# Halving the columns of each matmul in a streaming-encoder block: two passes over half of the tokens or output columns per weight unit

## The chip, the cores and the metric

The kernel runs on one core of a Trainium2 chip. The metric is the device time in microseconds of one execution, as the median of several runs. The core has a matrix engine (TensorE, PE in the rows; its weight loads stand apart as PEld), VectorE (DVE), ScalarE (ACT), GpSimd (POOL) and an engine for synchronisation that also issues transfers (SyncE, SP).

## The reference

One residual block in float32 for 512 tokens of width 2048:

```python
def hybrid_mixer(h, w_in, ...):
    proj = h @ w_in                       # q, k, v, forget logits, x_rnn, gate_rnn
    ...
    y_attn = forgetting_attention(q, k, v, log_f).reshape(B, S, D_ATTN)   # 16 heads x 64
    x_rnn = causal_dwconv(x_rnn, conv_rnn_w, conv_rnn_b)
    y_rnn = rg_lru(x_rnn, ...) * jax.nn.gelu(g_rnn)
    y = jnp.concatenate([rmsnorm(y_attn, norm_attn_out), rmsnorm(y_rnn, norm_rnn_out)], axis=-1)
    return y @ w_out

def conv_gated_mlp(h, w_gate, w_up, conv_ffn_w, conv_ffn_b, w_down):
    g = causal_dwconv(h @ w_gate, conv_ffn_w, conv_ffn_b)
    return (jax.nn.gelu(g) * (h @ w_up)) @ w_down       # hidden width 6144

h = rmsnorm(x, norm_mix_pre);  x = x + rmsnorm(hybrid_mixer(h, ...), norm_mix_post)
h = rmsnorm(x, norm_ffn_pre);  x = x + rmsnorm(conv_gated_mlp(h, ...), norm_ffn_post)
```

## The kernel before

Every operand of a large product is split into two parts of reduced precision, hi and lo, and `product` (its three matmuls are lines 1723 to 1725) adds hi x hi, hi x lo and lo x hi into one accumulation bank. A bank holds 128 rows by 512 columns.

Weights arrive in *units* of 128 x 1024 numbers: eight tiles of 128 x 128 (`UK = 8`). For each unit SyncE issues a transfer into `raw`, ScalarE makes the hi part (lines 561, 924 and 567, by stage), VectorE the lo part (lines 1015, 1589 and 1025) and signals `split_done`; TensorE waits for that, uses the unit and signals `unit_used`, which frees the split's buffer. Two buffers (three in the fast products) take turns.

The stages in order, with what TensorE does in each:

- the opening: 4 units in another order (`opening_unit`) and four direct calls of `unit`, which stay as they are
- the projection: for each of 8 pairs of heads five *tiles* of the output (k, q, the recurrent input, its gate, v; the order is written out by hand in `pair`). A `tile` is two units, one for each half of the input channels. In a unit a weight tile of 128 x 128 is the stationary side and 512 tokens of one channel tile (`act_hi`, `act_lo`) are the moving side: 8 products, 24 matmuls. Between tiles, and in the middle of some units (`middle`), stand the attention's scores, transposes and value products and the gates of the recurrence. Pair 1 is written out; pairs 2 to 7 are a loop, `pe.Fori(2, NP)`, with `NP = 8`
- the output projection: `out_opening` and one unit written out (unchanged), then `out_half` 27 times, 24 of them in a loop of 3 turns
- the feed-forward part: `OPEN` units that start four tiles at once (unchanged), 8 tiles by `tile`, and then the *fast products* for the other 42 hidden tiles: seven products of half size in place of eight, in which each matmul moves 256 tokens (`HS = 256`). They are unchanged
- the down projection: `down_unit`, 4 groups of 24 units. Here the tokens are stationary: for each of 4 blocks of 128 tokens (a bank each) and each of 2 hidden tiles (`kt`) the hidden activation `h_tokens` is loaded, and 512 output columns of the weights move. Each group's units 2 to 21 are a loop of ten turns; the last unit of all is `last_unit`, which goes bank by bank
- the end: norm, transposes back, residual and stores

## Time and profile before

| what | value |
|---|---|
| median of 3 runs | 2210.19 us (2208.95 to 2212.57) |
| the profiled execution | 2208.31 us |
| its span, first to last instruction | 2206.6 us |
| TensorE busy | 2188.2 us (99%), 13418 matmuls |
| weight loads busy | 1936.6 us (88%), 13418 loads |
| VectorE busy | 1530.0 us (69%) |
| ScalarE busy | 1002.1 us (45%) |
| mean granted TensorE clock | 0.999 |

Matmuls overlap in the pipeline, so TensorE's busy share says only that it was never empty. What one matmul costs is the distance from its start to the next one's.

### The profile page before, as it was taken

To read this page: it belongs to the slowest core of one execution; us is meant where nothing else is said; L and a number is where in the kernel's file an instruction comes from. 1 tells how busy PE (TensorE), PEld (TensorE's weight loads), DVE (VectorE), ACT (ScalarE), POOL (GpSimd) and SP (SyncE) were. 2 spreads that over 40 slices of the span, in tenths; PEclk is the share of its full clock that TensorE was granted. 3 is DMA by queue.
4 is the path that set the end of the run, shared out by engine and by line. 5 is a ranking of instruction groups with operands and counts; after the bars stand their busy time and mean duration, and the time that the engine had idled before them with its cause. 6 is when DMAs were issued, how large, how long until landed. Compare 5 with 4: busy or idle time off the path is not lost.

```text
span 2206.6 us, 34616 instructions
## 1 busy us (share of the span) xinstructions
PE 2188.2 (99%) x13418; PEld 1936.6 (88%) x13418; DVE 1530.0 (69%) x2022; ACT 1002.1 (45%) x1275; POOL 140.2 (6%) x207
## 2 busy tenths in 40 slices
PE   9999999999999999999999999999999999999998
PEld 7778888888788888999999999999997888888886
DVE  7776777778755887888888888888884444444445
ACT  5555555447322554444444444444443343343433
POOL 0000000000100001111111111111112000000000
PEclk9999999999999999999999999999999999999999
DMA  5222222222432436777777777777767322222243
GB/s 173 88 90 95 82 97 96 89 95 83 140 120 95 153 115 195 211 209 202 205 208 207 208 207 207 214 213 204 203 180 284 124 96 95 97 98 94 97 171 117
DMA packets 100397, 328.67 MB, mean 149 GB/s; under 512 B 12976, under 2 KB 20784, under 8 KB 100160
## 3 DMA queue, kind: packets, MB, share of 16 engines
q1 hardware_dynamic: 75456, 240.06, 31.5%
q0 software_dynamic: 22240, 82.36, 17.0%
q10 hardware_dynamic: 2592, 4.72, 0.6%
q8 instruction: 77, 1.26, 0.2%
q14 instruction: 32, 0.26, 0.0%
HBM read 306.09 MB, written 21.00 MB: 148 GB/s over the span
## 4 chain that ended last, share of the span: by engine, by line
PE 93%; DVE 4%; issue 2%; ACT 1%; DMA 1%; POOL 0%; DVEq 0%; ACTq 0%; SPq 0%; POOLq 0%
PE bank L1723 30%; PE bank L1725 30%; PE bank L1724 30%; PE bank L1782 1%; PE bank L1795 1%; DVE w_all L1015 1%; ACT w_all L561 0%; DVE x_b L1714 0%; DMA raw<-weights 0%; PE bank L1807 0%; PE bank L1806 0%; PE bank L1867 0%; DVE act_lo L1030 0%; PE bank L1753 0%; DMA h_t<-h_spill 0%
## 5 line engine op out<-in xcount | busy, mean ns | idle before, releaser
L1723 PE MATMUL bank<-act_hi,w_all 128*128 128x512 f32 (+1 forms) x1760 | 617.2, 351 | 3.5 <-DVE w_all L1015 2.2
L1725 PE MATMUL bank<-act_hi,w_all 128*128 128x512 f32 (+1 forms) x1760 | 612.3, 348 | 0.0
L1724 PE MATMUL bank<-act_lo,w_all 128*128 128x512 f32 (+1 forms) x1760 | 609.6, 346 | 0.0
L1723 PEld LDWEIGHTS bank<-act_hi,w_all 128*128 128x128 f32 x1760 | 330.6, 188 | 48.7 <-issue 2.8
L1725 PEld LDWEIGHTS bank<-act_hi,w_all 128*128 128x128 f32 x1760 | 330.5, 188 | 46.1
L1724 PEld LDWEIGHTS bank<-act_lo,w_all 128*128 128x128 f32 x1760 | 330.6, 188 | 43.8 <-issue 0.2
L1025 DVE TENSOR_TENSOR w_all<-raw,w_all 128x1024 fp32r<-128x1024 f32 x96 | 117.6, 1225 | 287.7 <-ACT w_all L567 287.7
L1723 PE MATMUL bank<-w_all,act_hi 128*128 128x512 f32 x768 | 302.8, 394 | 2.2 <-DVE w_all L1025 1.4
L1725 PE MATMUL bank<-w_all,act_lo 128*128 128x512 f32 x768 | 301.1, 392 | 0.0
L1724 PE MATMUL bank<-w_all,act_hi 128*128 128x512 f32 x768 | 298.1, 388 | 0.0
L1015 DVE TENSOR_TENSOR w_all<-raw,w_all 128x1024 fp32r<-128x1024 f32 x135 | 165.3, 1224 | 143.6 <-ACT w_all L561 141.9
L1723 PE MATMUL bank<-tsum,w_all 128*128 128x256 f32 x896 | 247.3, 276 | 0.0
L1724 PE MATMUL bank<-tsum,w_all 128*128 128x256 f32 x896 | 247.3, 276 | 0.0
L1725 PE MATMUL bank<-tsum,w_all 128*128 128x256 f32 x896 | 247.3, 276 | 0.0
L567 ACT ACTIVATE w_all<-raw 128x1024 fp32r<-128x1024 f32 x96 | 101.8, 1060 | 297.1 <-PE bank L1725 283.7
L561 ACT ACTIVATE w_all<-raw 128x1024 fp32r<-128x1024 f32 x135 | 142.5, 1056 | 178.0 <-PE bank L1725 177.8
L924 ACT ACTIVATE w_all<-raw_s 128x1024 fp32r<-128x1024 f32 x112 | 119.1, 1063 | 154.1 <-PE bank L1725 151.2
L1725 PEld LDWEIGHTS bank<-w_all,act_lo 128*128 128x128 f32 x768 | 144.1, 188 | 33.7
L1724 PEld LDWEIGHTS bank<-w_all,act_hi 128*128 128x128 f32 x768 | 144.2, 188 | 32.2
L1723 PEld LDWEIGHTS bank<-w_all,act_hi 128*128 128x128 f32 x768 | 144.4, 188 | 31.8 <-DVE w_all L1025 1.6
L1589 DVE TENSOR_TENSOR w_all<-raw_s,w_all 128x1024 fp32r<-128x1024 f32 x112 | 137.3, 1226 | 46.6 <-ACT w_all L924 45.4
L1724 PEld LDWEIGHTS bank<-tsum,w_all 128*128 128x128 f32 x896 | 168.2, 188 | 0.0
(274 smaller groups left out, 3687.5 us busy)
## 6 DMA issues: line engine op xcount, KB each, us to landing
raw<-weights SPq DMA_DIRECT2D x310, 512.0 KB, 3.5
raw_s<-weights SPq DMA_DIRECT2D x84, 512.0 KB, 4.5
raw_s<-weights POOLq DMA_DIRECT2D x84, 512.0 KB, 6.1
raw_a<-weights SPq DMA_DIRECT2D x42, 512.0 KB, 5.2
h_spill<-h_out POOLq DMA_DIRECT2D x48, 256.0 KB, 3.6
h_t<-h_spill POOLq DMA_DIRECT2D x24, 512.0 KB, 7.6
x<-xT POOLq DMA_DIRECT2D x16, 256.0 KB, 3.1
out<-x ACTq DMA_DIRECT2D x16, 256.0 KB, 2.8
```

What stands on the lines that cost most here:

```text
L561: act.activation(w_hi[s], raw[:, s], ACT.Copy).then_inc(hi_done, 1)
L567: act.activation(wd_hi[s], raw[:, s], ACT.Copy).then_inc(hi_done, 1)
L924: act.activation(w_slot(q)[0], RAW_OF[n](i), ACT.Copy).then_inc(hi_done, 1)
L1015: dve.tensor_tensor(w_lo[s], raw[:, s], word(w_hi[s]), ALU.subtract).then_inc(split_done, 1)
L1025: dve.tensor_tensor(wd_lo[s], raw[:, s], word(wd_hi[s]), ALU.subtract).then_inc(split_done, 1)
L1589: dve.tensor_tensor(lo, RAW_OF[n](i), word(hi), ALU.subtract).then_inc(split_done, 1)
L1723: pe.matmul(dst, ah, bh, start=start, stop=False, skip_group_check=goes_on)
L1724: pe.matmul(dst, ah, bl, start=False, stop=False, skip_group_check=goes_on)
L1725: return pe.matmul(dst, al, bh, start=False, stop=stop, skip_group_check=goes_on)
L1782: last[e] = pe.matmul(dst, q, k, start=t == 0, stop=t == 2)
L1795: last = pe.transpose(dst, sm[:, c:c + P], ident[:])
```

## The change

`unit_by_tokens` is new. It takes the place of `unit` in `tile` and `out_half`: the unit's eight products are run over tokens 0 to 255 and then over tokens 256 to 511, each time with all eight weight tiles; what stood in the middle of the unit now stands between the two passes. `down_unit` and `last_unit` go bank by bank, and in each bank over output columns 0 to 255, then 256 to 511. The arithmetic is the same; each matmul of 512 columns becomes two of 256 into the two halves of the same bank, and its weight tile is loaded twice.

```diff
+            def unit_by_tokens(u, s, half, bank, start, stop, middle=None):
+                pe.wait_ge(split_done, u + 1)
+                for n in range(2):
+                    c = slice(HS * n, HS * n + HS)
+                    if middle and n:
+                        middle()
+                    for i in range(UK):
+                        k = half * UK + i
+                        last = product(bank[:, c], w_tile(s, i), (act_hi[:, k, c], act_lo[:, k, c]),
+                                       start and n == 0 and i == 0, stop and n == 1 and i == UK - 1, True)
+                last.then_inc(unit_used, 1)
+
             def tile(u, bank, between=None, middle=None, middle2=None):
 
-                unit(u, 0, 0, bank, True, False, middle=middle)
+                unit_by_tokens(u, 0, 0, bank, True, False, middle)
                 if between:
                     between()
-                unit(u + 1, 1, 1, bank, False, True, middle=middle2)
+                unit_by_tokens(u + 1, 1, 1, bank, False, True, middle2)
...
             def out_half(t, s, half, middle=None):
                 u = t * 2 + (N_OUT + half)
-                unit(u, half, half, OUT_BANKS[s][half], True, True, middle=middle)
+                unit_by_tokens(u, half, half, OUT_BANKS[s][half], True, True, middle)
...
             def down_unit(n, s, out_banks, start=False, stop=False):
                 pe.wait_ge(split_done, n + (N_HID + 1))
                 pe.wait_ge(h_split, n + 1)
-                for kt in range(2):
-                    w = slice(S * kt, S * kt + S)
-                    for i, bank in enumerate(out_banks):
-                        last = product(bank[:], (h_tokens(act_hi, s, kt, i), h_tokens(act_lo, s, kt, i)),
-                                       (wd_hi[s][:, w], wd_lo[s][:, w]), start and kt == 0, stop and kt == 1)
+                for i, bank in enumerate(out_banks):
+                    for c in range(0, S, HS):
+                        for kt in range(2):
+                            w = slice(S * kt + c, S * kt + c + HS)
+                            last = product(bank[:, c:c + HS], (h_tokens(act_hi, s, kt, i), h_tokens(act_lo, s, kt, i)),
+                                           (wd_hi[s][:, w], wd_lo[s][:, w]), start and c == 0 and kt == 0,
+                                           stop and c > 0 and kt == 1, True)
                 last.then_inc(unit_used, 1)
```

`last_unit` is changed in the same way as `down_unit`.

The first place is TensorE's program in the pair loop, around the gates in the middle of a unit of the third tile, `tile(u + 4, SB[1])` (bank3 is the tile's bank, bank5 and bank6 the gates'; a row is a matmul, and its weight load isn't shown). Before:

```order
L1723 MATMUL bank3<-act_hi,w_all 128x512
L1724 MATMUL bank3<-act_lo,w_all 128x512
L1725 MATMUL bank3<-act_hi,w_all 128x512
L1723 MATMUL bank5<-xc_hi,gw_hi 128x512 [waits xc_split,gw_split,pt_split]
L1724 MATMUL bank5<-xc_lo,gw_hi 128x512
L1725 MATMUL bank5<-xc_hi,gw_lo 128x512
L1723 MATMUL bank6<-xc_hi,gw_hi 128x512
L1724 MATMUL bank6<-xc_lo,gw_hi 128x512
L1725 MATMUL bank6<-xc_hi,gw_lo 128x512
L1723 MATMUL bank3<-act_hi,w_all 128x512
L1724 MATMUL bank3<-act_lo,w_all 128x512
```

And the same place with the change:

```order
L1723 MATMUL bank3<-act_hi,w_all 128x256
L1724 MATMUL bank3<-act_lo,w_all 128x256
L1725 MATMUL bank3<-act_hi,w_all 128x256
L1723 MATMUL bank5<-xc_hi,gw_hi 128x512 [waits xc_split,gw_split,pt_split]
L1724 MATMUL bank5<-xc_lo,gw_hi 128x512
L1725 MATMUL bank5<-xc_hi,gw_lo 128x512
L1723 MATMUL bank6<-xc_hi,gw_hi 128x512
L1724 MATMUL bank6<-xc_lo,gw_hi 128x512
L1725 MATMUL bank6<-xc_hi,gw_lo 128x512
L1723 MATMUL bank3<-act_hi,w_all 128x256
L1724 MATMUL bank3<-act_lo,w_all 128x256
```

The gates keep their shape and place. Ahead of them 12 matmuls of 512 columns have become 24 of 256, and as many stand behind them. In the pair loop's body, matmuls go from 310 to 550, and the other 24 instructions (registers, waits, the branch) stay.

The second place is TensorE's program in the down projection, across the wait between the first and the second unit of the first group. Before:

```order
L1723 MATMUL bank3<-w_all,act_hi 128x512
L1724 MATMUL bank3<-w_all,act_hi 128x512
L1725 MATMUL bank3<-w_all,act_lo 128x512
L1723 MATMUL bank0<-w_all,act_hi 128x512 [waits h_split,split_done]
L1724 MATMUL bank0<-w_all,act_hi 128x512
L1725 MATMUL bank0<-w_all,act_lo 128x512
L1723 MATMUL bank1<-w_all,act_hi 128x512
```

With the change:

```order
L1723 MATMUL bank3<-w_all,act_hi 128x256
L1724 MATMUL bank3<-w_all,act_hi 128x256
L1725 MATMUL bank3<-w_all,act_lo 128x256
L1723 MATMUL bank0<-w_all,act_hi 128x256 [waits h_split,split_done]
L1724 MATMUL bank0<-w_all,act_hi 128x256
L1725 MATMUL bank0<-w_all,act_lo 128x256
L1723 MATMUL bank0<-w_all,act_hi 128x256
```

The unit starts at the same bank behind the same wait, but stays on it for four products (12 matmuls) before it goes to the next one, where it went on after one product. The programs of the other engines are the same in both kernels.

## Rows read from the trace of the kernel before

**Rows 1.** The page: span, busy time by engine, TensorE's granted clock by slice

```profile
span 2206.6 us, 34616 instructions
...
PE 2188.2 (99%) x13418; PEld 1936.6 (88%) x13418; DVE 1530.0 (69%) x2022; ACT 1002.1 (45%) x1275; POOL 140.2 (6%) x207
...
PEclk9999999999999999999999999999999999999999
```

**Rows 2.** The page: the chain that ended last, by engine

```profile
PE 93%; DVE 4%; issue 2%; ACT 1%; DMA 1%; POOL 0%; DVEq 0%; ACTq 0%; SPq 0%; POOLq 0%
```

**Rows 3.** The waits (total us, times, longest): TensorE's two longest, ScalarE's on TensorE

```profile
PE bank L1867 <- POOL ones L472: 2.4, 1, 2.4
PE bank L1723 <- DVE w_all L1015: 2.2, 3, 1.1
...
ACT w_all L567 <- PE bank L1725: 283.7, 93, 4.5
```

**Rows 4.** Groups by line and shape on TensorE (busy us, mean ns | idle)

```profile
L1723 PE MATMUL bank<-act_hi,w_all 128*128 128x512 f32 x1088 | 431.7, 397 | 3.5 <-DVE w_all L1015 2.2 <-DVE act_lo L1364 0.7 <-DVE act_lo L1030 0.6
...
L1725 PE MATMUL bank<-w_all,act_lo 128*128 128x512 f32 x768 | 301.1, 392 | 0.0
...
L1723 PE MATMUL bank<-tsum,w_all 128*128 128x256 f32 x896 | 247.3, 276 | 0.0
...
L1723 PE MATMUL bank<-act_hi,w_all 128*128 128x256 f32 x672 | 185.5, 276 | 0.0
```

**Rows 5.** Busy time in stretches: PE, PEld, DVE, ACT, POOL, clock, DMA share, GB/s

```profile
900.00:1600.00 700.00, 700.00 (x6179) 700.00 (x6178) 576.08 (x699) 328.30 (x368) 86.40 (x111) 1.00 0.77 207
1700.00:2100.00 400.00, 400.00 (x1749) 328.23 (x1748) 179.40 (x158) 155.45 (x170) 3.39 (x5) 1.00 0.31 105
...
254.60:318.48 63.88, 63.88 (x312) 52.85 (x312) 46.19 (x80) 32.99 (x53) 1.07 (x2) 1.00 0.27 92
```

**Rows 6.** The timeline, TensorE: first and last of two runs of seven

```profile
1399.78 0.28 PE L1723 MATMUL bank<-tsum,w 128*128 128x256 f32 x1
...
1400.46 0.28 PE L1723 MATMUL bank<-tsum,w 128*128 128x256 f32 x1
...
1999.81 0.39 PE L1723 MATMUL bank<-w_all,act_hi 128*128 128x512 f32 x1
...
2001.18 0.39 PE L1723 MATMUL bank<-w_all,act_hi 128*128 128x512 f32 x1
```

**Rows 7.** The chain in order of time: start, us, what

```profile
80.00 1.05 ACT w_all L561
...
123.80 0.47 PE bank L1723
...
137.38 1.09 PE bank L1795 x10
...
538.81 1.06 ACT w_all L561
...
562.35 0.50 PE bank L1723
```

**Rows 8.** DMA: instruction queues of the whole; 210:540 us; 900:1600 us; issues

```profile
q8 instruction: 77, 1.26, 0.2%
...
q1 hardware_dynamic: 8544, 27.27, 24.5%
q0 software_dynamic: 912, 3.15, 3.1%
...
q8 instruction: 49, 0.80, 0.4%
...
par<-params SPq DMA_DIRECT2D x1, 168.5 KB, 3.5
...
negc<-tt POOLq DMA_DIRECT2D x1, 32.0 KB, 2.0
```

More of the change, by code:

```diff
@@ L2096, in last_unit @@
                 for i, bank in enumerate(out_banks):
-                    for kt in range(2):
-                        w = slice(S * kt, S * kt + S)
-                        last = product(bank[:], (h_tokens(act_hi, s, kt, i), h_tokens(act_lo, s, kt, i)),
-                                       (wd_hi[s][:, w], wd_lo[s][:, w]), False, kt == 1)
+                    for c in range(0, S, HS):
+                        for kt in range(2):
+                            w = slice(S * kt + c, S * kt + c + HS)
+                            last = product(bank[:, c:c + HS], (h_tokens(act_hi, s, kt, i), h_tokens(act_lo, s, kt, i)),
+                                           (wd_hi[s][:, w], wd_lo[s][:, w]), False, c > 0 and kt == 1, True)
                     last.then_inc(last_done, 1)
```

## The prediction

> **What bounds the kernel now.** I read the page's table of busy time first. TensorE is busy for 2188.2 of 2206.6 us, with 13418 matmuls, and its granted clock is in the top tenth in all forty slices [rows 1]; of the two levels, 1.2 and 2.4 GHz, that is the upper one. The share alone proves little, so the chain that ended last comes next: 93% of it is TensorE [rows 2]. The waits say the same from both sides. TensorE's own waits are few, the two longest 2.4 and 2.2 us in total, while ScalarE, which makes the first half of each weight split, waited 93 times for TensorE in the down projection, up to 4.5 us at a time, in a unit of 24 matmuls that lasts 24 x 0.229 = 5.5 us [rows 3]. The time is the number of matmuls times the distance from one start to the next, and the change touches just this product.
>
> **What a matmul costs.** The groups by line show two shapes: 3 x (1088 + 768) = 5568 matmuls of 512 columns, and 256-column ones in the fast products (quadrants of the activation and sums of quadrants) [rows 4]. The "mean ns of one" (392 and 276) isn't their price, since they overlap. The price is the spacing. In 900 to 1600 us TensorE never pauses and 6179 matmuls of 256 columns reach into the stretch; in 1700 to 2100 us it is 1749 of 512 columns [rows 5]. A matmul is counted when any part of it lies in the window, so the starts cover the window and one duration: 700.28 / 6179 = 113.33 ns, and 400.39 / 1749 = 228.93 ns. The timeline agrees as far as its digits go: six matmuls from 1399.78 to 1400.46 (113 ns each) and six from 1999.81 to 2001.18 (228 ns) [rows 6]. Two short ones cost 226.66 ns, one long one 228.93 ns: the long one is **2.27 ns dearer** than the pair that replaces it, though the pair needs a second weight load. That load shows no price of its own: in 900 to 1600 us loads are as many as matmuls, one each 113 ns, under busier DMA (0.77 against 0.31) and a busier VectorE (82% against 45%) [rows 5]. So contention doesn't explain why the long ones are dearer.
>
> The Trainium skill, in "TensorE: Matmul & The Clock Gate", section "Back-to-back issue gap", speaks against the change: it gives a spacing of N/2.4 + 2.5 ns, so each matmul has a fixed part and halving pays it twice. By that rule two of 256 would cost 2 x 109.2 against 215.8, 2.5 ns more, and the sum below would be +12.7 us, or 2223 us. The trace disagrees in both size and sign: 113.33 and 228.93.
>
> **The change part by part.**
>
> 1. *Which matmuls are split.* `tile` and `out_half` now call `unit_by_tokens`. Tiles: 10 units in each of the pairs 1 to 7 and 2 units of the first pair's last tile, 72 units, 1728 matmuls; the 8 tiles of the feed-forward part, 16 units, 384; `out_half` 27 times, 648. `down_unit` and `last_unit`: 96 units of 8 products of 3, 2304. Sum 5064 of the 5568; the other 504 (openings, direct calls of `unit`, `out_opening`) stay. TensorE should then show 13418 + 5064 = 18482 matmuls.
> 2. *Their price.* 5064 x 2.27 ns = 11.5 us less. Reading the row counts at the edge of the windows without that one duration gives 2.1 ns and 10.7 us; one more matmul or one less in 1749 moves it by 0.13 ns, 0.7 us. I keep 10.5 to 12.5 for the pure spacing.
> 3. *Where a faster TensorE brings nothing.* The chain leaves TensorE for a long stretch twice while split matmuls run: from 80.00 to 123.80 us (ScalarE and VectorE in the pair written out ahead of the loop) and from 538.81 to 562.35 us (the last head's work and the split of y) [rows 7]. There TensorE only arrives earlier at its wait. At most 67.3 / 0.229 = 294 split matmuls lie there: 0.7 us of the gain is given back as waits for VectorE. Nothing is queued behind those waits on TensorE but the matmuls of the same stage. Remaining: 10.8 us.
> 4. *The middle of a unit.* `middle` (gates, scores, transposes) ran after 12 matmuls of 512 and now runs after 24 of 256, which is 2.75 against 2.72 us into the unit. Cost nothing; the cover is that neither half has a wait of its own.
> 5. *Order in the down projection.* Before, four banks took turns and all ended in the unit's last quarter; now each bank gets its 12 matmuls in one piece. `unit_used` is signalled at the unit's end in both. `last_unit` already went bank by bank, so VectorE and ScalarE get the last four banks in the same rhythm. Cost nothing. The stationary side (tokens of h) is the same 128 columns, loaded once more.
> 6. *Other engines.* Their programs don't change. The tightest steady stage is the pair loop: VectorE has 46.19 us of work in 63.88 us [rows 5]. With 240 split matmuls a turn it becomes 63.3 us, and 17 us of slack are left on VectorE and 30 on ScalarE. In the down projection weights must come twice 5.5 us apart; transfers are asked for by the splits, which wait for TensorE, so everything moves up with it.
> 7. *Waits held in registers.* In the loops each unit is preceded by a register instruction and a wait (10 units in 6 turns, 8 in 3, 2 in 40: 164 of them). Before, the loop's stretch has the plain spacing, so they hide behind the 229 ns matmuls. They now have 113 ns cover from a single matmul. If all of this cover were needed they would cost up to 164 x 0.115 = 19 us; the nearest row is the fast stretch, where a wait stands before each 24 matmuls of 256 (written out, not looped) and costs nothing. I take nothing, being nearer to that, and keep the other end for the range.
>
> Sum: the profiled execution took 2208.31 us around its span of 2206.6. 2208.31 - 10.8 = 2197.5 (span 2195.8). The median of the runs is 2210.19, 1.9 us above that execution, so the forecast for a median is **2199.4 us**, 0.5% faster.
>
> **The rivals.**
>
> *Code loading (slower).* The pair loop's body grows from 310 matmuls with their loads and 24 other instructions, 644, to 1124. An instruction takes 0.80 MB / 12357 = 65 bytes, and the queue for instructions brings 1.26 MB / 77 = 16.4 KB a packet [rows 8], so the body grows from 2.5 to 4.4 packets' worth. Today it stays on the chip: from 210 to 540 us, five turns, no row for that queue appears [rows 8]. If 4.4 packets' worth no longer stays, each jump back (5 in the pair loop, 2 in the output loop, whose body becomes 3.1) waits for a transfer. Small transfers took 2.0 us and 3.5 us from issue to landing [rows 8]: 7 x 2.0 to 3.5 = 14 to 25 us, which makes 2213 to 2224 us. It decides from 1.6 us a jump. For it: nothing in the trace shows how much stays. Against it: what must stay only grows by two packets, and straight code never waits for it.
>
> The Trainium skill disagrees with itself here: "Advanced Engine Details and Errata", section "ISA Cache", gives TensorE 128 KB, in which 72 KB fit, and the same place and "Runtime: NRT & Kernel Launch", section "Instruction fetch mechanics", speak of two lines of 16 KB, outside which a taken branch stalls. The 2.5 packets that stay today are more than two lines, so the trace sides against the second.
>
> *A fixed cost per matmul in these stages (slower).* The 512-column spacing is 15.6 ns above 512 / 2.4; the 256-column one 6.7 above 256 / 2.4. If in these stages the 15.6 ns belonged to each matmul, through its place in the program and not its width, two would cost 244.5 ns and the time would be 2210.19 + 5064 x 15.6 ns = 2289 us. For it: ten transposes of only 128 columns take 1.09 us on the chain, 109 ns each, almost what 256 columns take [rows 7]. Against it: 672 x 3 matmuls of 256 columns read the very tensors act and w_all that the units read [rows 4], at the small spacing. From 1.1 ns per matmul on the gain is gone. The rule of the Trainium skill's TensorE page that is quoted above is a rival of this kind; its 2223 us is its time here.
>
> *The gain is eaten in part.* Points 3 and 7 larger than I took them: register waits at a third of their bound, or VectorE's stretches growing longer since the pair before ends sooner. 2203 to 2210, say 2206 us.
>
> *No effect.* That the change does nothing is excluded: the shapes change, and time can stay only if the costs cancel.
>
> **How the numbers follow.** Forecast 0.78, at 2199.4 with its own range of 2196 to 2202.5 (10.5 to 12.5 by spacing, and the runs' own scatter of about 2 us). Partly eaten 0.10. Code loading 0.07. Fixed cost 0.05. The range of 2195.5 to 2207.5 holds nearly all of the first and most of the second. A difference of under 0.2%, 4.4 us, can't be told from none: faster (under 2205.8) takes the first case and a third of the second, 0.81; same the rest of the second, 0.07; slower the last two, 0.12.
>
> **What would show it.** Right: in a stretch of the down projection 113.3 ns from start to start, some 3530 matmuls over 400 us where 1749 were; pair loop turns of 63.3 us in place of 63.88; granted clock unchanged; TensorE waits 0.7 us longer in all; some 90 instruction packets in place of 77. Wrong: instruction packets inside the pair loop and a pause of 2 us at its turns (code loading); a spacing above 114.5 ns in the units though the fast products stay at 113.3 (fixed cost); pauses at unit starts in loops only (register waits). If the long matmul's 228.93 ns came from the stage and not from its width, the spacing in the units would be half of it, 114.5 ns, and the time wouldn't move.

## The result: 1.2% slower, and the profile after

| what | value |
|---|---|
| median of 4 runs | 2236.26 us (2236.04 to 2237.01), before 2210.19 |
| ratio to before | 1.0116, 95% interval 1.0104 to 1.0128 |
| span of the profiled execution | 2234.4 us (27.8 longer) |
| mean granted TensorE clock | 0.999, as before |

The forecast was 2199.4 us. The page of the changed kernel answers to [rows 1, 2]:

```profile
span 2234.4 us, 44744 instructions
...
PE 2215.9 (99%) x18482; PEld 2176.5 (97%) x18482; DVE 1530.1 (68%) x2022; ACT 1002.7 (45%) x1275; POOL 140.5 (6%) x207
...
PEclk9999999999999999999999999999999999999999
...
q8 instruction: 91, 1.49, 0.3%
...
PE 92%; DVE 4%; issue 2%; ACT 1%; DMA 1%; SPq 0%; POOL 0%; DVEq 0%; ACTq 0%; POOLq 0%
```

The number of matmuls is the one forecast, VectorE and ScalarE do the work of before in the time of before, and the clock stayed at its upper level. The one large difference is in the weight loads: 88% before, 97% now. TensorE's waits are hardly longer than in [rows 3]:

```profile
PE bank L1723 <- DVE w_all L1025: 2.5, 1, 2.5
PE bank L1882 <- POOL ones L472: 2.4, 1, 2.4
PE bank L1723 <- DVE w_all L1015: 2.3, 3, 1.1
```

So the loss isn't in a wait, and must be in the spacing. The windows answer to [rows 5] (columns: stretch, its length, then busy time and count of PE, PEld, DVE, ACT and POOL, clock, DMA share, GB/s):

```profile
143.00:161.00 18.00, 18.00 (x161) 18.00 (x161) 10.61 (x22) 7.62 (x14) 0.54 (x1) 1.00 0.38 117
...
600.00:700.00 100.00, 100.00 (x852) 100.00 (x851) 53.67 (x69) 25.22 (x28) 3.23 (x6) 1.00 0.35 111
900.00:1600.00 700.00, 700.00 (x6179) 700.00 (x6178) 575.18 (x700) 328.78 (x367) 86.50 (x111) 1.00 0.79 208
1676.00:1685.00 9.00, 9.00 (x82) 9.00 (x81) 3.94 (x6) 2.09 (x3) 0.00 (x0) 1.00 1.03 393
1700.00:2100.00 400.00, 400.00 (x3398) 400.00 (x3398) 173.44 (x153) 149.36 (x164) 4.99 (x7) 1.00 0.32 103
256.83:321.51 64.68, 64.68 (x553) 63.84 (x552) 46.18 (x80) 33.11 (x53) 1.07 (x2) 1.00 0.30 91
```

With the counting of the prediction (a matmul lasts 0.28 us in these rows), the fast products still stand at 700.28 / 6179 = 113.33 ns. The down projection does not: 400.28 / 3398 = 117.80 ns, where 3530 matmuls were forecast. The output projection from 600 to 700 us has 100.28 / 852 = 117.70. Yet 143 to 161 us of the first pair, 18.28 / 161 = 113.5 (with the edges' roundness of one matmul, 0.7), and the first two units of the down projection, 9.28 / 82 = 113.2, have the shorter spacing in matmuls of the same lines and tiles. The pair loop's turn is 321.51 - 256.83 = 64.68 us instead of 63.88.

The timeline shows the two side by side, at the start of the third unit of the down projection (start, us):

```profile
1685.63 0.28 PE L1723 MATMUL bank<-w_all,act_hi 128*128 128x256 f32 x1
1685.74 0.28 PE L1724 MATMUL bank<-w_all,act_hi 128*128 128x256 f32 x1
1685.86 0.28 PE L1725 MATMUL bank<-w_all,act_lo 128*128 128x256 f32 x1
1686.42 0.38 PE L1723 MATMUL bank<-w_all,act_hi 128*128 128x256 f32 x1 [0.29 <-DVE act_lo L1019]
1686.64 0.28 PE L1724 MATMUL bank<-w_all,act_hi 128*128 128x256 f32 x1
1686.76 0.28 PE L1725 MATMUL bank<-w_all,act_lo 128*128 128x256 f32 x1
1686.88 0.28 PE L1723 MATMUL bank<-w_all,act_hi 128*128 128x256 f32 x1
...
1687.94 0.28 PE L1723 MATMUL bank<-w_all,act_hi 128*128 128x256 f32 x1
```

Ahead of the wait the starts lie 113 ns apart; behind it nine starts take 1687.94 - 1686.88 = 1.06 us, 118 ns each. Lines, tiles and shapes are the same on both sides, and the 118 ns go on to the end of the projection.

A matmul of 256 columns thus has **two spacings**, 113.3 and 117.8 ns. A pair at the shorter costs 226.7 ns, 2.27 less than one of 512 columns; a pair at the longer costs 235.6 ns, 6.7 *more*. Which of the two holds decides the sign. The time adds up with it: if all 5064 pairs had the longer spacing, the loss would be 5064 x 6.67 = 33.8 us. By the starts in the trace, each of the seven pairs of heads from the first on has one stretch at the shorter: six of 168 matmuls (84 pairs of matmuls each) and a last one of 72 (36), and in the down projection 96 have it (48). For 588 pairs x 8.94 ns that is 5.3 us less, so 28.5 us; the span grew by 27.8.

By stage, from starts in the two timelines: the fast products begin at 872.65 us instead of 860.19 (12.5 later), last from there to their last start 799.57 in both kernels (1672.22 - 872.65, 1659.76 - 860.19), and the down projection takes 2217.82 - 1674.98 = 542.8 us from its first start to its last instead of 2189.96 - 1661.45 = 528.5 (14.3 longer). Another 1.1 us is a longer wait ahead of it, for VectorE. The last starts, in the changed kernel and before:

```profile
2217.82 0.28 PE L1725 MATMUL bank<-w_all,act_lo 128*128 128x256 f32 x1
```

```profile
2189.96 0.40 PE L1725 MATMUL bank<-w_all,act_lo 128*128 128x512 f32 x1
```

### The profile page after: what moved, and what is told of

It is laid out like the page before. It is cut to its first block, busy times and chain, and to the rows that moved or that the text cites. A ratio compares the mean times of both kernels' runs of the same rounds, so it can differ in the third digit from the quotient of the medians.

```text
span 2234.4 us, 44744 instructions
## 1 busy us (share of the span) xinstructions
PE 2215.9 (99%) x18482; PEld 2176.5 (97%) x18482; DVE 1530.1 (68%) x2022; ACT 1002.7 (45%) x1275; POOL 140.5 (6%) x207
## 4 chain that ended last, share of the span: by engine, by line
PE 92%; DVE 4%; issue 2%; ACT 1%; DMA 1%; SPq 0%; POOL 0%; DVEq 0%; ACTq 0%; POOLq 0%
PE bank L1725 30%; PE bank L1723 30%; PE bank L1724 29%; DMA raw<-weights 1%; PE bank L1797 1%; DVE w_all L1015 1%; PE bank L1810 1%; ACT w_all L561 0%; DVE x_b L1714 0%; PE bank L1822 0%; DVE act_lo L1030 0%; PE bank L1821 0%; DMA h_t<-h_spill 0%; PE bank L1768 0%; DVE pt_lo L1109 0%
## 5 line engine op out<-in xcount | busy, mean ns | idle before, releaser
L1723 PE MATMUL bank<-act_hi,w_all 128*128 128x256 f32 (+1 forms) x2680 | 769.1, 287 | 3.6 <-DVE w_all L1015 2.3
L1725 PE MATMUL bank<-act_hi,w_all 128*128 128x256 f32 (+1 forms) x2680 | 764.0, 285 | 0.0
L1724 PE MATMUL bank<-act_lo,w_all 128*128 128x256 f32 (+1 forms) x2680 | 763.7, 285 | 0.0
L1723 PEld LDWEIGHTS bank<-act_hi,w_all 128*128 128x128 f32 x2680 | 502.9, 188 | 14.4 <-DVE w_all L1015 2.8
L1725 PEld LDWEIGHTS bank<-act_hi,w_all 128*128 128x128 f32 x2680 | 503.3, 188 | 6.9
L1724 PEld LDWEIGHTS bank<-act_lo,w_all 128*128 128x128 f32 x2680 | 502.8, 188 | 7.1 <-issue 0.2
L1723 PE MATMUL bank<-w_all,act_hi 128*128 128x256 f32 x1536 | 428.7, 279 | 2.8 <-DVE w_all L1025 2.5
L1725 PE MATMUL bank<-w_all,act_lo 128*128 128x256 f32 x1536 | 429.9, 280 | 0.0
L1724 PE MATMUL bank<-w_all,act_hi 128*128 128x256 f32 x1536 | 428.4, 279 | 0.0
L1025 DVE TENSOR_TENSOR w_all<-raw,w_all 128x1024 fp32r<-128x1024 f32 x96 | 117.7, 1226 | 301.6 <-ACT w_all L567 301.6
L1723 PEld LDWEIGHTS bank<-w_all,act_hi 128*128 128x128 f32 x1536 | 287.3, 187 | 3.2 <-DVE w_all L1025 2.7
L1724 PEld LDWEIGHTS bank<-w_all,act_hi 128*128 128x128 f32 x1536 | 288.8, 188 | 0.0
L1725 PEld LDWEIGHTS bank<-w_all,act_lo 128*128 128x128 f32 x1536 | 288.3, 188 | 0.0
```

Source lines behind the costliest of these rows:

```text
L1025: dve.tensor_tensor(wd_lo[s], raw[:, s], word(wd_hi[s]), ALU.subtract).then_inc(split_done, 1)
L1723: pe.matmul(dst, ah, bh, start=start, stop=False, skip_group_check=goes_on)
L1724: pe.matmul(dst, ah, bl, start=False, stop=False, skip_group_check=goes_on)
L1725: return pe.matmul(dst, al, bh, start=False, stop=stop, skip_group_check=goes_on)
```

## The experiments

The theories, in words: the matmul of 256 columns has two spacings and the units run at the longer one (the first theory of the expectations; with variants on what ahead of a stretch sets it); or the loss comes from a particular part of the change (passes, order in the down projection), from reading the same tensors that other engines write (contention), from the place in the program, or from semaphore waits. All kernels are made from the changed one; times of before are those of the same chip.

**One half of the change each.** `e1_tiles_only` keeps `down_unit` and `last_unit` of before; `e2_down_only` keeps `unit` in `tile` and `out_half`:

```diff
# e1
-                for i, bank in enumerate(out_banks):
-                    for c in range(0, S, HS):
...
+                for kt in range(2):
+                    w = slice(S * kt, S * kt + S)
# e2
-                unit_by_tokens(u, 0, 0, bank, True, False, middle)
+                unit(u, 0, 0, bank, True, False, middle=middle)
```

> Edit: the tiles and the output projection run by halves of the tokens as in the change; the down projection stays as before (512 columns). Theory 1 (two rhythms): a 256-column matmul runs either 113.3 or 117.8 ns from the next, and most of the changed units are in the slower one. 2760 long matmuls of 228.9 ns become 5520, of which 7 stretches of 168 ran at 113.3 in the changed kernel: 2760 x 6.7 ns less 1176 x 4.4 ns is 13 us, so about 2223 us. Theory 2 (the loss sits in the down projection alone, by its new bank order): 2210 us or less.

> Edit: the down projection as in the change; the tiles and the output projection as before. Theory 1: 2304 x 6.7 ns = 15 us more, less 0.4 us for the 96 matmuls at 113.3: about 2225 us, and the down projection at 117.8 ns a matmul but for its first two units. Theory 2 (losses add up only because both are changed, for instance by the code size): near 2210 us.

Measured: e1 2222.09 us, before 2209.11, ratio 1.0059 (1.0042 to 1.0075). e2 2223.39, ratio 1.0062 (1.0046 to 1.0079). Both halves lose, 13.0 and 14.3 us, 27.3 together, about the whole loss of 26 to 28 us: two losses of the same kind that add up, so no single place in the program is to blame. e2's windows hold a surprise:

```profile
1700.00:2100.00 400.00, 400.00 (x3399) 400.00 (x3398) 174.85 (x154) 151.42 (x166) 3.56 (x5) 1.00 0.32 100
2132.00:2200.00 68.00, 68.00 (x602) 68.00 (x602) 30.16 (x29) 25.70 (x27) 0.00 (x0) 1.00 0.27 85
```

From the eleventh unit of the last group on, behind a pause of 0.1 us at 2129.9 us, the spacing is 68.28 / 602 = 113.4 ns to the end (671 matmuls), while the changed kernel has the longer spacing in the same code (74 us from 2131 hold 631 matmuls, 117.7 ns).

**What a width costs.** `e3_forms` and `e8_widths` give feed-forward tiles 2 to 8 other cuts of their 512 columns (four tiles in e3, six in e8), each unit still once over all its weights per cut. The last of the seven keeps 256 and 256, and two tiles of e3 keep 256 columns in another order. Both kernels also take other orders in the groups of the down projection.

```diff
# e8
-            tile(N_FF + 12, PT[2])
+            tile_form(N_FF + 12, PT[2], ("cols", (0, 224, 512)))
-            tile(N_FF + 14, SB[2])
+            tile_form(N_FF + 14, SB[2], ("cols", (0, 248, 512)))
```

> Edit: the changed kernel with another form in each of the feed-forward tiles 2 to 8 (4 x 128 columns; 384 and 128; 448 and 64; 320 and 192; halves inside each product; halves inside each single matmul with the same weight tile twice in a row; 256 as in the change) and in each group of the down projection (512 as before; as in the change; both halves of a product one behind the other; all banks' first halves, then the second). Theory 1: every 256-column form shows 117.8 or 113.3 ns and nothing between, whatever its order, and which of the two changes at borders of units. Theory 2 (the order of banks and halves costs): the form whose order is that of before is at 113.3 or 114.5, the change's order alone at 117.8. The other widths show where the spacing stops following the columns: 128 columns near 109 to 113 ns if the weight load sets the floor, near 57 ns if the columns do.

> Edit: the changed kernel with other widths in the feed-forward tiles 2 to 8 (240 and 272; 224 and 288; 248 and 264; 208 and 304; 192, 192 and 128; 32 and 480; 256 and 256) and, by group of the down projection, both halves of a product one behind the other; all banks' first halves, then the second; as in the change; 512 columns. The run of other forms gave 108 to 112 ns up to 192 columns, and 15.5 ns above the column time (columns / 2.4) for 320 to 512. Theory 1: 256 columns lie where a floor of some 108 to 113 ns by the weight load meets the columns' line (106.7 + 15.6 = 122.3 ns), so widths up to 248 are at 108 to 113, and from 264 up (125.6, 129, 135.6, 142.3 ns) they follow the line. Theory 5 (15.6 ns is a cost of wide matmuls only): 264 to 304 columns at 6.7 ns above the column time (117 to 133 ns).

Measured once each: 2250.87 us (before 2209.11) and 2249.05 (2210.28). The whole times mix the forms; the spacings are what counts. In e8's timeline, the first start of each run of 24 matmuls of one width:

```profile
804.77 0.26 PE L1723 MATMUL bank<-act_hi,w_all 128*128 128x224 f32 x1
...
807.44 0.31 PE L1723 MATMUL bank<-act_hi,w_all 128*128 128x288 f32 x1
...
810.65 0.27 PE L1723 MATMUL bank<-act_hi,w_all 128*128 128x224 f32 x1
...
816.53 0.28 PE L1723 MATMUL bank<-act_hi,w_all 128*128 128x248 f32 x1
...
819.25 0.28 PE L1723 MATMUL bank<-act_hi,w_all 128*128 128x264 f32 x1
...
822.17 0.27 PE L1723 MATMUL bank<-act_hi,w_all 128*128 128x248 f32 x1
```

The difference of two starts divided by 24: 224 columns 111.3 ns, 248 113.3, 264 121.7, 288 133.8. The rest from the same two traces: 128 columns 111 to 112, 192 111, 208 110.8, 304 141.7, 384 175.4, and 512 stays at 228.9. So there are two regimes. Up to 248 columns the spacing is nearly a floor of 111 to 113 ns, whatever the width. Above 256 columns it is the columns at the upper clock level plus a fixed part: 264 / 2.4 + 11.7, 288 / 2.4 + 13.8, 384 / 2.4 + 15.4, 512 / 2.4 + 15.6. The width 256 stands at the corner, and its two spacings fit the two regimes: 113.3 is the floor as at 248, and 117.8 is 256 / 2.4 + 11.1, on the line to 264. The fixed part of the long matmul belongs to the matmul, and a pair pays it twice unless both run on the floor. That this is what the two spacings are is argued from the widths, not shown by itself.

e3 shows something else. Its last three tiles, with 256 columns in three orders, stand behind the tile of 320 and 192 columns, and all of them have the shorter spacing; its three groups of 256 columns in the down projection, in three orders too, have the longer one (PE, clock, DMA share, GB/s):

```profile
857.00:888.00 31.00, 31.00 (x276) 1.00 0.58 167
...
1840.00:2220.00 380.00, 379.26 (x3221) 1.00 0.32 103
```

31.28 / 276 = 113.3 ns, and 379.5 / 3221 = 117.8 (one pause taken off). The order sets neither.

The Trainium skill, "TensorE: Matmul & The Clock Gate", section "LDWEIGHTS (loading the stationary operand)", gives a load P / 1.2 ns, 106.7 for 128 columns, which is also 256 / 2.4. The floor measured here is 4 to 7 ns above that, and the loads' busy share of 97% in the changed kernel goes with it; that the loads set the floor is argued, no run takes them away. The rule that the prediction weighed, N / 2.4 + 2.5 in "Back-to-back issue gap" of the same page of the Trainium skill, is given there for an isolated matmul. It has the right sign; the constant is 11 to 16 ns in these traces.

**What moves a stretch from one spacing to the other.** `e4_nudge` puts small things ahead of units: one or two matmuls of ones, transposes, a first product cut in two (in the down projection at the heads of the second group, at 128 columns, and of the fourth, at 64).

```diff
+                            if cut and i == 0 and c == 0 and kt == 0:
+                                for c0, c1 in ((0, cut), (cut, HS)):
+                                    product(bank[:, c0:c1], (h_tokens(act_hi, s, kt, i), h_tokens(act_lo, s, kt, i)),
+                                            (wd_hi[s][:, c0:c1], wd_lo[s][:, c0:c1]), start and c0 == 0, False, True)
+                                continue
```

> Edit: the changed kernel with a small disturbance ahead of the feed-forward tiles 2 to 8 (one and two matmuls of ones, the first product cut at column 128 and at 64, one, four and ten transposes of 128 columns) and at the head of the down projection's groups 2 and 4 (first product cut at 128 and at 64). The order of the rest is the same. Theory 1 (two rhythms of the same stream, entered by the history of the pipeline): at least one disturbance moves the following matmuls from 117.8 to 113.3 ns, and they stay there until the next border. Theory 3 (the spacing is a property of the stage: its tensors, banks or what the other engines do there): every tile stays at 117.8.

Measured once: 2227.33 us, 9 less than the changed kernel, with more matmuls. In the feed-forward tiles no nudge changed anything. In the down projection (columns: PE, clock, DMA share, GB/s):

```profile
1700.00:1800.00 100.00, 100.00 (x851) 1.00 0.40 136
1820.00:2060.00 240.00, 240.00 (x2120) 1.00 0.30 96
2080.00:2130.00 50.00, 50.00 (x427) 1.00 0.48 175
```

Ahead of the first cut 100.28 / 851 = 117.8 ns, behind it 240.28 / 2120 = 113.3 through two whole groups, and behind the second cut 50.28 / 427 = 117.8 again. That lasts until a wait for VectorE at 2132 us, behind which the last 671 matmuls are at the shorter one, as in e2:

```profile
2134.00:2208.00 74.00, 74.00 (x656) 1.00 0.26 83
```

74.28 / 656 = 113.2 ns. A spacing is a **state that keeps itself up** through 2300 matmuls, waits in registers and banks changing, until something disturbs it.

`e5_lead_320` puts a product of 320 and 192 columns ahead in each unit, as what stood ahead of the three tiles of e3, in the expectation that it sets the shorter spacing.

```diff
+                for c in (slice(0, 320), slice(320, S)):
+                    product(bank[:, c], w_tile(s, 0), (act_hi[:, k, c], act_lo[:, k, c]), start and c.start == 0, False, True)
```

> Edit: the changed kernel, but each changed unit begins with its first product cut at column 320 (320 and 192 columns) and goes on by halves. In the run of other forms the stream was at 113.3 ns behind a tile of 320 and 192 columns. Theory 1a (the matmuls of 192 columns at the head bring the stream into the faster rhythm and it stays): most of the units at 113.3 ns, the time near 2200 us (2197 plus 211 heads that cost some 20 ns more each = 4 us). Theory 1b (the rhythm is drawn at each restart whatever stands ahead): a mix of both, 2205 to 2240 us. Theory 3 (a property of the stage): 117.8 throughout, 2240 us.

Measured: 2262.16 us, ratio 1.0234 (1.0217 to 1.0251). The matmuls of 256 columns in the units stayed at 117.8 ns, but for 21 in each of three turns of the pair loop, and there the next product of 320 columns ended the shorter spacing. That variant fell. The time lies above all the expectations, because the odd product costs more than the 20 ns put down for it. By the spacings of 320 columns (148.9 ns, the mean of e3's two runs of them) and 192 it is an estimated 3 x (148.9 + 111) - 6 x 117.8 = 73 ns, 15 us for 211 units; with the 5.3 us of the stretches at the shorter spacing that are gone, 5 of the 26 us stay unexplained.

**Contention, place, order, waits.** `e6_quiet_down` lets the splits of the down projection, from the third unit on, make one column instead of 1024: VectorE's and ScalarE's work there goes, and the output isn't the reference's.

```diff
-                act.activation(wd_hi[s], raw[:, s], ACT.Copy).then_inc(hi_done, 1)
+                c = slice(None) if isinstance(n, int) and n < 2 else slice(0, 1)
+                act.activation(wd_hi[s][:, c], raw[:, s, c], ACT.Copy).then_inc(hi_done, 1)
```

> Edit: the changed kernel; in the down projection the splits of all weights and hidden tiles but the first two units' make one column in place of all (so the output is not the reference's from there on); the transfers and signals stay. VectorE and ScalarE are nearly idle there, and the splits are ready early. Theory 3 (other engines' reads and writes stretch the 256-column matmuls to 117.8 ns): the down projection at 113.3 ns, 20 us less than the changed kernel, 2216 us. Theory 1: 117.8 or 113.3 as the entry falls, a group as a whole, and no spacing between the two; the 563 ns wait behind the second unit is gone, and if a wait is what moves the stream to the slower rhythm it stays at 113.3 until the next disturbance.

Measured once: 2235.51 us, and the longer spacing from the first unit of the down projection on. VectorE is busy for 29.27 us of 400 instead of 173.44, ScalarE 30.61 instead of 149.36, and TensorE has the same 3399 matmuls:

```profile
1700.00:2100.00 400.00, 400.00 (x3399) 400.00 (x3398) 29.27 (x154) 30.61 (x164) 4.26 (x6) 1.00 0.32 102
```

`e7_shift` runs 25 instead of 18 matmuls of ones at the very start; the program behind is the changed kernel's.

```diff
-            keep_busy(18, PT[2])
+            keep_busy(25, PT[2])
```

> Edit: the changed kernel with 25 in place of 18 matmuls of ones in the idle time ahead of the first product. Nothing else. Theory 1 (the rhythm falls with the timing of restarts): the stretches at 113.3 and at 117.8 ns may lie at other places than in the changed kernel, in steps of whole stretches; time within 2225 to 2240 us. Theory 4 (each place in the program has its own spacing, for instance by its address in the instruction stream): the same stretches as in the changed kernel, since the instructions behind move by 7 only; time 2236 us.

Measured once: 2239.23 us. The stretches that have the shorter spacing are others. The first feed-forward tile by `tile`, 783 to 797 us, in this kernel and then in the changed one:

```profile
783.00:797.00 14.00, 14.00 (x126) 1.00 0.25 78
```

```profile
783.00:797.00 14.00, 14.00 (x121) 1.00 0.35 105
```

14.28 / 126 = 113.3 ns against 14.28 / 121 = 118.0, in the same instructions. In turn the first two units of the down projection, and the first pair's stretch from 143 us, have the longer spacing in e7. So the place in the program alone doesn't choose. It isn't without effect, though: in the loop's six turns, in e7 and in each of the ten other profiled kernels whose pair loop runs its tiles in 256 columns alone, the shorter spacing begins behind the same four transposes and holds up to the next ones (168 matmuls, 72 in the last turn). Behind the same transposes in the first pair, ahead of the loop, it is there in eight of these kernels and missing in e4, e7 and e12. In e12, whose edit comes much later, TensorE's instructions up to there are those of the changed kernel, which has 161 matmuls in this window:

```profile
143.00:161.00 18.00, 18.00 (x155) 1.00 0.34 110
```

`e9_halves_inner` runs both halves of the columns in each product before the next weight tile; `e10_same_weights_twice` goes further, two halves behind each other on the same weights; `e11_wait_each_24` adds a semaphore wait in the middle of each unit, as the fast products have it at each 24 matmuls.

```diff
# e9
-                for n in range(2):
...
+                for i in range(UK):
...
+                    for n in range(2):
# e10
+                        for n in range(2):
+                            c = slice(HS * n, HS * n + HS)
+                            last = pe.matmul(bank[:, c], w, a[:, k, c], start=start and i == 0 and j == 0 and n == 0,
# e11
+                    if n:
+                        pe.wait_ge(split_done, u + 1)
```

> Edit: as the changed kernel, but the two halves of a product stand one behind the other (three matmuls of the first half, three of the second), in the tiles, the output and the down projection. The same number of 256-column matmuls. Theory 1 (two rhythms, fallen into at restarts, not by order): 113.3 and 117.8 ns again, in other stretches than in the changed kernel; anything from 2198 us (all fast) to 2239 us (all slow). Theory 6 (this order is what was fast in the run of other forms): 113.3 nearly throughout, 2198 to 2203 us.

> Edit: as before, but each weight tile's load is followed by its second use at once: hi x hi on both halves, then hi x lo on both, then lo x hi. Each matmul still loads its own. Theory 1: as for the run ahead, 2198 to 2239 us. Theory 7 (loading the tile that is already there costs less): below 113.3 ns a matmul, under 2195 us.

> Edit: the changed kernel with the unit's wait written a second time ahead of its second pass, so that a wait stands before each 24 matmuls, as in the fast products (which ran at 113.3 ns in every run so far). Theory 8 (that regular wait keeps the stream in the faster rhythm): the tiles and the output projection at 113.3 ns, the down projection as in the changed kernel; about 2219 us. Theory 1: no such effect, 2225 to 2240 us.

Measured: 2234.88 (ratio 1.0109, 1.0092 to 1.0126), 2236.60 (1.0119, 1.0102 to 1.0136), and once 2235.18 us. All three have 851 or 852 matmuls from 600 to 700 us and 3398 or 3399 from 1700 to 2100, as the changed kernel. Order, loading the same weights again, and waits that are met already don't matter; each trace is one execution, and e9's four runs, from 2231.97 to 2236.99 us, leave room for a stretch at the shorter spacing in some.

**Are the fast products immune?** `e12_disturb_fast` puts wide matmuls or transposes into the fast products of five of the 42 hidden tiles.

```diff
+                if n == 2 and i in (14, 32):
+                    for _ in range(2 if i == 14 else 8):
+                        pe.transpose(wide[:, 0:P], ident[:], ident[:])
+                if n == 2 and i == 26:
+                    for _ in range(3):
+                        product(wide[:, 0:320], (hi[:, 0:P], lo[:, 0:P]), (act_hi[:, 0, 0:320], act_lo[:, 0, 0:320]), True, True, True)
```

> Edit: the changed kernel with extra matmuls, whose results are overwritten, inside the fast products: one product of 512 columns ahead of the third product of tile 8, two transposes at 14, eight products of 512 at 20, three of 320 at 26, eight transposes at 32. Theory 1 (the fast products are at 113.3 ns because nothing disturbs them once they are there): behind one or more of these the stream is at 117.8 ns and stays there up to the next one, 504 matmuls x 4.4 ns = 2.2 us for each six tiles. Theory 9 (the fast products' own operands hold them at 113.3 ns): 113.3 within a few matmuls behind each disturbance; only the extra matmuls' own time, some 8 us, is added to the changed kernel's 2236 us.

Measured once: 2246.33 us. The products of 512 columns left the spacing as it was. Two transposes brought the next 46 matmuls to 117.8 ns, and with the first matmul on the third buffer (`w` in the names, where the others are `w_all`) it was 113.3 again:

```profile
1145.83 0.28 PE L1724 MATMUL bank<-tsum,w_all 128*128 128x256 f32 x1
...
1151.25 0.28 PE L1725 MATMUL bank<-tsum,w_all 128*128 128x256 f32 x1
1151.36 0.28 PE L1723 MATMUL bank<-act_hi,w 128*128 128x256 f32 x1
```

46 starts in 1151.25 - 1145.83 = 5.42 us, 117.8 ns each. Behind the 320-column products and behind the eight transposes it was 117.8 ns too, for 115 and 114 matmuls:

```profile
1381.50:1395.00 13.50, 13.50 (x117) 1.00 0.75 206
1497.00:1510.00 13.00, 13.00 (x113) 1.00 0.81 227
```

Both ended at a border onto `w` as well (1395.37 and 1511.02 us), but at the second; the first one (1386.88, 1502.54) they passed unchanged. So the fast products aren't of another kind. In every profiled kernel in which the longer spacing reached them it ended exactly at a border onto `w`: at the first one in the changed kernel (872.65 us), e1, e7 and e9 to e12, at the second in e4, e5, e6, e8 and e14. e6 has the changed kernel's instructions on TensorE throughout, passed the first border and turned at the second:

```profile
881.37 0.28 PE L1729 MATMUL bank<-tsum,w_all 128*128 128x256 f32 x1
881.49 0.28 PE L1727 MATMUL bank<-tsum,w 128*128 128x256 f32 x1
```

The units, with two buffers, have no such border. What about it does this stays open.

**Can the shorter spacing be had?** From e2, with units 2 to 5 of the first group written out: `e13_cut_once` cuts the first product of unit 4 at 128 columns, `e14_cut_heads` also those at the heads of the other three groups (the cut as in e4), `e15_no_cut` none.

```diff
+                if g == 0:
+                    first = 3
...
+                    down_unit(4, 0, out_banks, cut=128)
```

> The down projection split as in the change, tiles as before; in its first group units 2 to 5 are written out ahead of the loop, and the first product of unit 4 is cut into two of 128 columns (3 matmuls more). If such a cut brings the matmuls behind it from 117.8 to 113.3 ns, and nothing turns them back, some 3800 matmuls win 4.45 ns each against the same kernel without the cut (2223.4 us): 2206 to 2208 us, 0.1% faster than before. If the cut does nothing (the turn seen in the nudged kernel was chance), 117.8 ns goes on and the time stays at 2221 to 2224 us.

> The same, and the first product of groups 2, 3 and 4 is cut at 128 columns too. If a cut sets 113.3 ns whatever the spacing was, about 2207 us, 113.3 ns all along. If a cut turns the spacing over each time, groups 1 and 3 run at 113.3 and groups 2 and 4 at 117.8 ns (some 1150 matmuls each): near 2217 us. If cuts do nothing, 2221 to 2224 us.

> The same code as the first of these with no cut: control. 117.8 ns from about the third unit on, 2221 to 2224 us; if writing the units out is enough to change the spacing, it shows here.

Measured, before 2208.86 us: e15 2223.37 us (ratio 1.0070, 1.0055 to 1.0084). e13's twelve runs fall into two groups with nothing between them, six from 2207.96 to 2211.15 and six from 2223.80 to 2226.20, close to the expectations of both theories, in one kernel. e14's ten runs lie from 2210.51 to 2215.91 (median 2212.86, ratio 1.0019, 1.0010 to 1.0028). The profiled runs, behind the cut: in e13

```profile
1687.05 0.33 PE L1723 MATMUL bank<-w_all,act_hi 128*128 128x256 f32 x1
1687.22 0.28 PE L1724 MATMUL bank<-w_all,act_hi 128*128 128x256 f32 x1
...
1687.93 0.28 PE L1724 MATMUL bank<-w_all,act_hi 128*128 128x256 f32 x1
...
1700.00:2100.00 400.00, 400.00 (x3398) 400.00 (x3398) 174.21 (x154) 150.06 (x166) 3.56 (x5) 1.00 0.33 100
```

and in e14

```profile
1687.95 0.33 PE L1723 MATMUL bank<-w_all,act_hi 128*128 128x256 f32 x1
1688.12 0.28 PE L1724 MATMUL bank<-w_all,act_hi 128*128 128x256 f32 x1
...
1688.80 0.28 PE L1724 MATMUL bank<-w_all,act_hi 128*128 128x256 f32 x1
...
1700.00:2100.00 400.00, 400.00 (x3532) 400.00 (x3531) 181.53 (x160) 156.32 (x171) 4.11 (x6) 1.00 0.34 105
```

Same instructions, same start behind the cut (0.17 us to the second matmul), then six starts in 0.71 us in the one and in 0.68 in the other, and 117.8 against 400.28 / 3532 = 113.33 ns for the 400 us that follow. So a cut sets neither spacing. Behind the one of e13 the times say that each came in half of the runs, though only one of them, a longer one, was profiled; without a cut none of the eight runs of e2 and e15 was under 2220 us. e14 offers the chance four times, and its ten runs spread over 5.4 us, about what one group at the longer spacing costs (1150 x 4.45 ns = 5.1 us); a cut at 128 columns would then leave the shorter spacing alone and end the longer one now and then, which is argued from the times, one profile being all that shows it (e4's cut at 64 ended the shorter one). None of the three expectations for e14 named this time. In that profile the shorter spacing holds all through from the first cut on, and the forecast's price is seen at work: the down projection takes 2190.57 - 1663.92 = 526.7 us from first to last start against 528.5 before. The forecast's 2304 x 2.27 ns are 5.2 us; the four units ahead of the cut (0.9), the cuts (an estimated 1.3) and a wait of 1.3 us for VectorE at 2112.9 us take 3.5 of them. Even so e14 isn't faster than before: in this execution the down projection began 2.5 us later (1663.92 against 1661.45), behind tiles whose instructions are those of before. No version that beats it came out of these runs.

## Why the prediction was wrong

The step that failed is point 2, *their price*: "Two short ones cost 226.66 ns, one long one 228.93 ns" took the spacing of 256 columns from the fast products and gave it to the units as a property of the width. It is right for the fast products (6179 again) and wrong for most of the 10128 new matmuls: 117.8 ns. A price of -2.27 ns a pair became +6.7, and -11.5 us became +28.5.

- Point 1, which are split: right, 18482 matmuls.
- Point 3, gain given back at ScalarE's and VectorE's stretches: there was no gain to give back. The wait ahead of the down projection grew by 1.1 us.
- Points 4 and 5, the middle and the order, at nothing: right as far as it can be told; e3, e9 and e10 order the work otherwise and have the same spacings.
- Point 6, other engines not the bound: right; e6 takes most of their work away, and the spacing stays.
- Point 7, waits in registers at nothing: right. The loops show no pause at them, and e11's added waits cost nothing.
- The rival *code loading*: refuted. 91 packets of instructions (some 90 were forecast), and between 210 and 540 us, in a loop of 4.4 packets' worth, no row for that queue, as in [rows 8]; the queues in that stretch of the changed kernel are

```profile
q1 hardware_dynamic: 8000, 26.74, 25.9%
q0 software_dynamic: 912, 3.15, 3.1%
```

- The rival *a fixed cost per matmul in these stages*, at 0.05: what happened has its direction and its mark in the trace, "a spacing above 114.5 ns in the units though the fast products stay at 113.3". Its size, 15.6 ns, was off, and so was its reason: not the stage, since both spacings occur in the units as in the fast products (e2, e4, e12). What speaks against it in the prediction, that the fast products read the same tensors, was true and didn't bear on it.

What could have warned from the trace of before: one width was known at one spacing only, from one stage, in a steady stream; and 128-column transposes at 109 ns, nearly as dear as 256 columns [rows 7], said that below some width the matmul isn't what is paid for. 256 columns lie just where both meet, and a price taken at such a corner holds on one side only.

Open: what in the hardware holds the state and what draws it. Excluded by runs as what decides alone: contention with the splits, place, order within a unit, reloading, waits that are met, the instructions ahead (e6 and e12 against the changed kernel). Seen where it changed: transposes, 320 columns, a cut product, a pause, a border onto `w`. None of them changes it each time, and by the times the same cut went both ways in the same kernel.

## What to carry to other kernels

Don't split a stream of 512-column matmuls into 256 for the sake of a spacing that another stage shows: each matmul above the floor of about 113 ns carries 11 to 16 ns of its own, and at 256 columns these runs show it hidden in some stretches and paid in others, with no edit that settled which. When a difference of 1% per instruction is to carry a forecast, take the spacing from several stages and stretches, and look for a second value of it. A kernel whose runs fall into two groups may owe it to such a state of TensorE; count matmuls per 100 us before looking for waits.

## What the runs showed of the hardware

- 256-column matmuls with a weight load each keep one of two spacings, 113.3 or 117.8 ns, for up to thousands of instructions (3398 and 3532 in 400 us of one program).
- The same program can take either: e13 has runs 15 us apart (medians of its two groups 2210.0 and 2225.2). An estimate: the 3744 matmuls from the cut to the eleventh unit of the last group x 4.45 ns = 16.7 us.
- Below 248 columns the width hardly matters: 128 to 224 columns cost 111 to 112 ns (e3, e8).
- The same instructions took either spacing in two kernels: the first pair from 143 to 161 us holds 161 matmuls in the changed kernel and 155 in e12; the fast products turn to the shorter at the first border onto `w` in the changed kernel and at the second in e6.
- In e7, behind a stretch from 1670 to 1676 us in which TensorE was busy for 4.21 of 6 us, the granted clock was 0.63 on average from 1676.5 to 1681 us, partly at the lower of its levels, and 1.00 from 1682. The changed kernel was busy for 3.51 of the same 6 us and had 1.00 there. At the lower level e7's 256-column matmuls start 213 ns apart, which is 256 / 1.2 with nothing on top.
